# Second RMS norm of a decoder layer moved behind the gate and up products, its squares added by GpSimd, the first two output units interleaved

## The chip, the cores and the metric

One Trainium2 chip; the program runs on one of its cores. The metric is the time of one execution on the device in microseconds, here the median of three runs.

## What is computed

A two-layer hybrid decoder trunk on 320 tokens (256 of a prompt, 64 new ones of eight sequences), model width 1024. Each layer projects the normed input, runs three token mixers (a linear recurrence, latent attention over a paged cache, a gated chunk mixer), merges them with sigmoid gates, adds the result of an output projection to x, and then runs a SwiGLU feed-forward network of width 2816. The change is in this last part:

```python
x = x + jnp.sum(gates * proj, axis=2) @ lp['w_out']
hf = rms_norm(x, lp['ffn_norm'])     # x * rsqrt(mean(x*x) + EPS) * g
x = x + (jax.nn.silu(hf @ lp['w_gate']) * (hf @ lp['w_up'])) @ lp['w_down']
```

## The kernel before

Everything is feature-major: x is held as 8 tiles of 128 features by 320 tokens (KT = 8, T = 320). Each weight matrix is streamed in units of 128 x 1024 values, 129 per layer, through three slots (SLOTS). For every unit SyncE loads it into `raw`, ScalarE copies it rounded into `w_hi` and VectorE subtracts to get `w_lo` (both called `split` in the code; each is a fixed place in its engine's program). TensorE forms a product as three passes (w_hi with a_hi, w_hi with a_lo, w_lo with a_hi), so a full unit is 8 x 3 matmuls of 128 x 320, and it needs its operand a in two parts as well, a high part from ScalarE and a low part from VectorE. The split of unit u may start when unit u - 3 is done on TensorE.

The order on each engine is the order of its program; semaphores join them. The part of a layer that the change touches (`ffn` of each engine) runs as follows.

Output units (U_E, 8 of them): TensorE multiplies the merged tiles `mg_hi`, `mg_lo` by w_out, unit after unit, into PSUM banks 0 to 3. For each m, VectorE splits unit m + 2, adds the bank to x[m] (L2079) and frees the bank; ScalarE splits unit m + 2, waits for x[m] and writes its square into `tmpf`. For m = 0 TensorE waits for each merged tile in turn.

Norm (`norm(l, 1, tmpf)`): TensorE multiplies the 8 squares by a matrix of ones into bank 4 (L736), ScalarE makes rb = exp(-0.5 ln(mean + eps)) from it, each of the two functions behind a table load; VectorE multiplies x[m], the gain and rb into `tmpf` (L1686), ScalarE copies pairs of tiles into `h_hi`, VectorE subtracts into `h_lo` (L1626), and TensorE starts unit U_F, two tiles at a time as they come (`first_unit`).

Gate and up units (U_F, 44 of them, 22 pairs; a loop of 7 rounds of 3 pairs and one pair behind it): of a pair, ScalarE takes tanh of the gate unit's bank (`fth`), VectorE forms (fth + 1) x gate bank and then x up bank (`fhd`), ScalarE copies this into `hid_hi`, VectorE subtracts into `hid_lo` (each the L1182 or L1626 helper). Between these steps stand the splits of the two units ahead. The gate bank is freed after the (fth + 1) step, the up bank after the last product.

Down units (U_G, 22): each adds one hidden tile's product into all 8 banks, so that the first of them waits bank by bank for a free one; behind them VectorE adds the banks to x.

GpSimd has nothing to do in these stages; its next work is to load the vectors of the next layer.

Of the kernel before, what the change touches and what calls it, by code (L numbers as in the profile page):

```python
# [21 lines left out]
T = SEQ + TS  # L22
# [44 lines left out]
def build_program(nc, ins, outs):  # L67
# [116 lines left out]
    fhd = sb("fhd", [128, 2, T], on=st5)  # L184
    st5.close()
# [170 lines left out]
    ff_p = Signal("ffn_product", NF)  # L356
# [177 lines left out]
    def _(pool):  # L534
        nc.gpsimd.memset(ones[:], 1.0).then_inc(consts_set.sem, 1)

        with pool.Fori(0, DEPTH) as l:
# [152 lines left out]
            for q in (NB - 2, NB - 1):  # L690
                for m in range(NPG // 2):
                    if m % 2 == 0:
                        split_probabilities(q, m // 2)
                    rows_lo(q, m)


    @block.tensor
    def _(pe):
# [22 lines left out]
        def first_unit(l, u, slot, bank, n):  # L721

            pe.wait_ge(lo_done.sem, lo_done.at(l, u + 1))
            pe.wait_ge(bank_free[bank].sem, banks.take(l, bank))
            for j in range(KT // 2):
                pe.wait_ge(h_ready.sem, h_ready.at(l, 4 * n + j + 1))
# [4 lines left out]
        def norm(l, n, tmp):  # L731

            pe.wait_ge(bank_free[4].sem, banks.take(l, 4))
            for m in range(KT):
                pe.wait_ge(sq_ready.sem, sq_ready.at(l, n * KT + m + 1))
                last = mm(PS[:, 4, 0:T], ones[:], tmp[:, m, :], start=m == 0, stop=m == KT - 1)  # L736
            last.then_inc(norm_sum.sem, 1)
# [6 lines left out]
        def project(l):  # L744
            norm(l, 0, tmp8)
            first_unit(l, 0, 0, 0, 0)
# [377 lines left out]
        def ffn(l):  # L1124
            for m in range(KT):
                pe.wait_ge(lo_done.sem, lo_done.at(l, U_E + m + 1))
                pe.wait_ge(bank_free[m % 4].sem, banks.take(l, m % 4))
                for k in range(KT):
# [4 lines left out]
                done.then_inc(unit_done.sem, 1)  # L1133
            norm(l, 1, tmpf)
            with pe.Fori(0, 7) as i:
                banks.enter(i, [0, 1, 2, 3, 5, 6])
                first_unit(l, i * 6 + U_F, U_F % SLOTS, 0, 1)
                for j, b in ((1, 1), (2, 2), (3, 3), (4, 5), (5, 6)):
                    full_unit(l, i * 6 + (U_F + j), (U_F + j) % SLOTS, b)
                banks.leave(7)  # L1140
            for j in (42, 43):
                full_unit(l, U_F + j, (U_F + j) % SLOTS, j - 42)
# [37 lines left out]
    def _(act):  # L1180
# [20 lines left out]
        def norm(l, n, tmp):  # L1201
            if n == 0:
                split(l, 0)
            for m in range(KT):
                act.wait_ge(x_ready.sem, x_ready.at(l, n * KT + m + 1))
                A(tmp[:, m, :], x[:, m, :], ACT.Square).then_inc(sq_ready.sem, 1)
            act.wait_ge(norm_sum.sem, norm_sum.at(l, n + 1))
            rs(rb[:], PS[:, 4, 0:T], D).then_inc(rb_ready.sem, 1)
            release(4)
            if n == 0:  # L1210
                split(l, 1)
            for j in range(4):
                act.wait_ge(ht_ready.sem, ht_ready.at(l, 4 * n + j + 1))
                A(h_hi[:, 2 * j:2 * j + 2, :], tmp[:, 2 * j:2 * j + 2, :], ACT.Copy).then_inc(hh_ready.sem, 1)
            if n == 0:
                act.wait_ge(par_abs.sem, par_abs.at(l, 1))
                A(sm(S_E, 0, 4), sm(S_E, 0, 4), ACT.Exp, scale=-1.0).then_inc(par_exp.sem, 1)
# [24 lines left out]
        def project(l):  # L1242
            norm(l, 0, tmp8)
# [321 lines left out]
        def ffn(l):  # L1565
            for m in range(KT):
                split(l, U_E + m + 2)
                act.wait_ge(x_ready.sem, x_ready.at(l, KT + m + 1))
                if m == 0:
                    act.wait_ge(mgh.sem, mgh.at(l, 8))  # L1570
                A(tmpf[:, m, :], x[:, m, :], ACT.Square).then_inc(sq_ready.sem, 1)
            act.wait_ge(norm_sum.sem, norm_sum.at(l, 2))
            rs(rb[:], PS[:, 4, 0:T], D).then_inc(rb_ready.sem, 1)
            release(4)
            for j in range(4):
                act.wait_ge(ht_ready.sem, ht_ready.at(l, 4 + j + 1))
                A(h_hi[:, 2 * j:2 * j + 2, :], tmpf[:, 2 * j:2 * j + 2, :], ACT.Copy).then_inc(hh_ready.sem, 1)

            def hidden(fi, c, i, step, bank, s):

                u = i * step + c
                split(l, c + 2, i, step)
# [7 lines left out]

            with act.Fori(0, 7) as i:
                for j in range(3):
                    hidden(i * 3 + j, U_F + 2 * j, i, 6, (0, 2, 5)[j], j % 2)
            hidden(21, U_F + 42, 0, 0, 0, 0)
# [18 lines left out]
    def _(dve):  # L1613
# [59 lines left out]
        def norm(l, n, tmp, gain):  # L1673
            if n == 0:
                split(l, 0)
            if n == 0:
                dve.wait_ge(vec_in.sem, vec_in.at(l, 16))
            dve.wait_ge(rb_ready.sem, rb_ready.at(l, n + 1))

            def pair_lo(j):  # L1680
                dve.wait_ge(hh_ready.sem, hh_ready.at(l, 4 * n + j + 1))
                lo(h_lo[:, 2 * j:2 * j + 2, :], tmp[:, 2 * j:2 * j + 2, :], h_hi[:, 2 * j:2 * j + 2, :]).then_inc(h_ready.sem, 1)

            for j in range(4):
                for m in (2 * j, 2 * j + 1):
                    last = V.scalar_tensor_tensor(tmp[:, m, :], x[:, m, :], v(gain, m), rb[:], ALU.mult, ALU.mult)  # L1686
# [4 lines left out]
            if n == 0:  # L1691
                split(l, 1)
                lru_parameters(l)

        def project(l):

            norm(l, 0, tmp8, "attn_g")
# [581 lines left out]
```

## Time and profile before

| | us |
|---|---|
| median of three runs | 1702.2 (1700.59 to 1705.34) |
| profiled execution, its own time | 1704.65 |
| span of that execution in the trace | 1703.1 |
| TensorE matmul busy, of the span | 1611.5 (95%) |
| TensorE weight load busy | 1537.3 (90%) |
| VectorE busy | 1029.7 (60%) |
| ScalarE busy | 941.2 (55%) |
| GpSimd busy | 458.7 (27%) |
| mean granted TensorE clock | 0.986 of full |

A busy share is the share of the span in which an instruction of that engine ran. The span is that of the trace, 1.55 us shorter than the execution's own time. Matmuls are pipelined: one lasts 0.31 us and the next starts 0.147 us after it, so that busy time alone doesn't say how close TensorE is to its pace; the idle stretches before its instructions do.

### The profile page before, as it was taken

The numbers are of one execution on the slowest core, as the hardware profiler recorded it, in microseconds if no ns is written. First come the engines' busy times: TensorE is split into PE (matmuls) and PEld (weight loads), VectorE is DVE, ScalarE is ACT, GpSimd is POOL, SyncE is SP. The second block draws the span as 40 slices with busy tenths as digits, with TensorE's granted clock in tenths as the row PEclk, the third lists the DMA queues.
The fourth block names the chain that finished last, engine by engine and source line by source line (L and its number), as shares of the span: only waits on it lengthen the run. The fifth ranks groups of instructions, "written<-read, shape, count | busy, mean of one in ns | idle before, by whom it ended". The sixth has DMA issues, their size and how long they took to land.

```text
span 1703.1 us, 34614 instructions
## 1 busy us (share of the span) xinstructions
PE 1611.5 (95%) x10896; PEld 1537.3 (90%) x10896; DVE 1029.7 (60%) x1557; ACT 941.2 (55%) x1654; POOL 458.7 (27%) x519
## 2 busy tenths in 40 slices
PE   7988999999999989999989889999999999899998
PEld 6875999999999989999978669999999999899998
DVE  5566777778543655554375567777784536555533
ACT  6585777777634344443366947776775343444331
POOL 1113356766620000000012223667666100000000
PEclk9999999999999999999999989999999999999999
DMA  6321355444444434444444123645435444344443
GB/s 228 116 71 50 113 181 155 148 147 142 149 142 135 158 106 152 150 150 149 136 148 127 48 63 119 188 142 155 150 122 179 125 138 160 105 151 150 149 148 105
DMA packets 113795, 232.02 MB, mean 136 GB/s; under 512 B 12801, under 2 KB 78402, under 8 KB 113410
## 3 DMA queue, kind: packets, MB, share of 16 engines
q1 hardware_dynamic: 111458, 222.94, 41.8%
q0 software_dynamic: 2208, 7.51, 1.3%
q8 instruction: 64, 1.05, 0.3%
q14 instruction: 65, 0.53, 0.1%
HBM read 227.93 MB, written 2.46 MB: 135 GB/s over the span
## 4 chain that ended last, share of the span: by engine, by line
PE 72%; ACT 9%; DVE 6%; issue 5%; DVEq 3%; ACTq 3%; POOLq 1%; DMA 0%; POOL 0%; SPq 0%
PE PS L711 45%; PE PS L955 18%; ACT L1182 2%; PE PS L988 1%; PE PS L989 1%; PE PS L950 1%; PE PS L736 1%; ACT lt_hi L1182 1%; ACTq L1186 1%; ACT ksqp L1182 1%; DVEq L1709 1%; DVEq L1617 1%; ACT r_hi L1182 1%; DVE xc L1711 1%; POOLq L652 1%
## 5 line engine op out<-in xcount | busy, mean ns | idle before, releaser
L1623 DVE TENSOR_TENSOR w_lo<-raw,w_hi 128x1024 fp32r<-128x1024 f32 x258 | 317.0, 1229 | 287.7 <-ACT w_hi L1182 274.8
L711 PE MATMUL PS<-h_hi,w_hi 128*128 128x320 f32 x1360 | 429.9, 316 | 31.3 <-DVE h_lo L1626 20.8
L711 PE MATMUL PS<-h_lo,w_hi 128*128 128x320 f32 x1360 | 424.8, 312 | 0.0
L711 PE MATMUL PS<-h_hi,w_lo 128*128 128x320 f32 x1360 | 424.6, 312 | 0.0
L1182 ACT ACTIVATE w_hi<-raw 128x1024 fp32r<-128x1024 f32 x258 | 272.0, 1055 | 161.9 <-PE PS L711 134.4
L711 PEld LDWEIGHTS PS<-h_hi,w_hi 128*128 128x128 f32 x1360 | 259.3, 191 | 40.5 <-issue 17.1
L711 PEld LDWEIGHTS PS<-h_lo,w_hi 128*128 128x128 f32 x1360 | 259.8, 191 | 0.3
L711 PEld LDWEIGHTS PS<-h_hi,w_lo 128*128 128x128 f32 x1360 | 259.4, 191 | 0.0
L955 PE MATMUL PS<-comb_hi,lt_hi 128*128 128x288 f32 x1024 | 240.2, 315 | 0.0
L1182 ACT ACTIVATE ksqp<-PS 128x512 f32<-128x512 f32 x256 | 152.5, 596 | 145.4 <-PE PS L955 143.1
L1969 DVE TENSOR_REDUCE kss<-ksqp 128x8 f32<-128x512 f32 x256 | 172.8, 680 | 96.6 <-ACT ksqp L1182 96.2
L955 PE MATMUL PS<-comb_lo,lt_hi 128*128 128x288 f32 x1024 | 218.7, 295 | 0.0
L955 PE MATMUL PS<-comb_hi,lt_lo 128*128 128x288 f32 x1024 | 218.6, 294 | 0.0
L660 POOL TENSOR_TENSOR r_lo<-rrow,r_hi 128x512 fp32r<-128x512 f32 x128 | 167.1, 1309 | 114.7 <-ACT r_hi L1182 114.6
L955 PEld LDWEIGHTS PS<-comb_lo,lt_hi 128*128 128x128 f32 x1024 | 164.1, 188 | 0.0
L955 PEld LDWEIGHTS PS<-comb_hi,lt_lo 128*128 128x128 f32 x1024 | 163.8, 188 | 0.0
L955 PEld LDWEIGHTS PS<-comb_hi,lt_hi 128*128 128x128 f32 x1024 | 159.1, 189 | 0.0
L639 POOL TENSOR_TENSOR lt_hi<-tpage,lt_hi 64x256 fp32r<-64x256 f32 x128 | 120.5, 942 | 94.3 <-ACT lt_hi L1182 77.8
L1626 DVE TENSOR_TENSOR lt_lo<-tpage,lt_hi 128x512 fp32r<-128x512 f32 x128 | 107.4, 839 | 24.5 <-ACT lt_hi L1182 24.5
L1182 ACT ACTIVATE lt_hi<-tpage 128x768 fp32r<-128x768 f32 x128 | 108.3, 846 | 2.3 <-DMA tpage<-in_tcache 2.3
L711 PE MATMUL PS<-hid_hi,w_hi 128*128 (+1 forms) x352 | 108.5, 308 | 0.4 <-DVEq L1617 0.4
L711 PE MATMUL PS<-hid_lo,w_hi 128*128 (+1 forms) x352 | 108.3, 308 | 0.0
(293 smaller groups left out, 2646.3 us busy)
## 6 DMA issues: line engine op xcount, KB each, us to landing
raw<-in_stream SPq DMA_DIRECT2D x258, 512.0 KB, 3.5
tpage<-in_tcache SPq DMA_DIRECT2D x256, 192.0 KB, 2.4
rrow<-in_rcache SPq DMA_DIRECT2D x256, 128.0 KB, 2.6
x<-in_xT SPq DMA_DIRECT2D x2, 640.0 KB, 5.4
sbias<-in_sbias POOLq DMA_DIRECT2D x2, 640.0 KB, 6.0
out_yT<-x SPq DMA_DIRECT2D x1, 1280.0 KB, 4.5
const<-in_consts SPq DMA_DIRECT2D x1, 1088.0 KB
wgate<-in_wgate POOLq DMA_DIRECT2D x2, 512.0 KB, 3.8
```

The costliest lines, as they stand in the source:

```text
L639: nc.gpsimd.tensor_tensor(half, tpage[64:128, c % TBUF, :, 256:384], f(half), ALU.subtract).then_inc(pt_rope.sem, 1)
L652: pool.drain()
L660: nc.gpsimd.tensor_tensor(r_lo[:, at, :], rrow[:, src, :], f(r_hi[:, at, 0:KVL]), ALU.subtract).then_inc(rows_split.sem, 1)
L711: done = mm(out, w[:, slot, c], a, start=first and n == 0 and m == 0, stop=last and n == len(pairs) - 1 and m == 2)
L736: last = mm(PS[:, 4, 0:T], ones[:], tmp[:, m, :], start=m == 0, stop=m == KT - 1)
L950: mm(PS[:, rotary_bank(p, par), r0:r0 + HT], lt_hi[:, t, i, 256:384], q128_of(b), start=True, stop=True)
L955: last = mm(PS[:, 2 * s + g, c0:c0 + 288], a[:, t, i, 128 * k:128 * k + 128], w[:, k, g, c0:c0 + 288], start=k == 0 and n == 0, stop=k == ...
L988: mm(PS[:, 7, 0:KVL], w, r_lo[:, r, :], start=False, stop=False)
L1182: return nc.scalar.activation(out, in_, func, **kw)
L1623: V.tensor_tensor(w_lo[:, s, :], raw[:, s, :], f(w_hi[:, s, :]), ALU.subtract).then_inc(lo_done.sem, 1)
L1626: return V.tensor_tensor(out, whole, f(hi_), ALU.subtract)
L1969: V.tensor_reduce(kss[:, par, p, :], ksqp[:, s, :].rearrange("p (h c) -> p h c", h=H), AX.X, ALU.add).then_inc(pk_ss.sem, 1)
```

## The change

1. The operand of gate and up products is no longer the normed x but x times the gain alone: ScalarE writes `h_hi[m]` from x[m] with the gain as the scale, as soon as x[m] is there, ahead of the square; VectorE writes `h_lo[m]` = x[m] x gain - h_hi[m] in one instruction, behind the split of the next turn. h_ready counts 8 tiles, not 4 pairs.
2. TensorE runs unit U_F straight behind the output units, tile by tile, then the sum of squares, then U_F + 1, then the loop. The squares of tiles 1 to 6 are added onto that of tile 0 by GpSimd, so that TensorE has two products with the ones instead of eight.
3. The token's norm rb is applied to the banks: VectorE writes fgs = gate bank x rb and, later, fus = up bank x rb, and the hidden value is (fth + 1) x fgs x fus. The tanh reads fgs instead of the bank, so ScalarE waits for VectorE twice in a pair (`ff_p` counts two per pair).
4. The first pair stands ahead of the loop, not behind it, and the banks rotate accordingly.
5. The first two output units are interleaved: tiles 0 to 3 of both, then tiles 4 to 7 of both.

The core of the diff (ScalarE's and TensorE's other `norm` only loses its parameters):

```diff
 # GpSimd, behind the pages of the layer
+            pool.wait_ge(sq_ready.sem, sq_ready.at(l, KT + 1))
+            pool.sem_inc(waits_passed, 1)
+            for m in range(1, KT - 1):
+                pool.wait_ge(sq_ready.sem, sq_ready.at(l, KT + m + 1))
+                pool.sem_inc(waits_passed, 1)
+                nc.gpsimd.tensor_tensor(tmpf[:, 0, :], tmpf[:, 0, :], tmpf[:, m, :], ALU.add)
+                last = pool.drain()
+            last.then_inc(sq_added.sem, 1)
 # TensorE, ffn
+            for m in (0, 1):
+                output_unit_ready(m)
+                merged_product(m, range(0, 4))
+            for m in (0, 1):
+                merged_product(m, range(4, KT)).then_inc(unit_done.sem, 1)
+            for m in range(2, KT):
+                output_unit_ready(m)
+                merged_product(m, range(KT)).then_inc(unit_done.sem, 1)
+            pe.wait_ge(lo_done.sem, lo_done.at(l, U_F + 1))
+            pe.wait_ge(bank_free[0].sem, banks.take(l, 0))
+            for k in range(KT):
+                pe.wait_ge(h_ready.sem, h_ready.at(l, 4 + k + 1))
+                done = tiles(PS[:, 0, 0:T], U_F % SLOTS, [(k, h_hi[:, k, :], h_lo[:, k, :])], first=k == 0, last=k == KT - 1)
+            done.then_inc(unit_done.sem, 1)
+            pe.wait_ge(bank_free[4].sem, banks.take(l, 4))
+            pe.wait_ge(sq_added.sem, sq_added.at(l, 1))
+            mm(PS[:, 4, 0:T], ones[:], tmpf[:, 0, :], start=True, stop=False)
+            pe.wait_ge(sq_ready.sem, sq_ready.at(l, 2 * KT))
+            mm(PS[:, 4, 0:T], ones[:], tmpf[:, KT - 1, :], start=False, stop=True).then_inc(norm_sum.sem, 1)
+            full_unit(l, U_F + 1, (U_F + 1) % SLOTS, 1)
 # ScalarE, ffn
+                A(h_hi[:, m, :], x[:, m, :], ACT.Copy, scale=v("ffn_g", m)).then_inc(hh_ready.sem, 1)
                 A(tmpf[:, m, :], x[:, m, :], ACT.Square).then_inc(sq_ready.sem, 1)
+            split(l, U_F + 2)
             act.wait_ge(norm_sum.sem, norm_sum.at(l, 2))
             rs(rb[:], PS[:, 4, 0:T], D).then_inc(rb_ready.sem, 1)
 # ScalarE, hidden
-                act.wait_ge(unit_done.sem, unit_done.at(l, u + 1))
-                A(fth[:, s, :], PS[:, bank, 0:T], ACT.Tanh, scale=0.5).then_inc(ff_t.sem, 1)
+                act.wait_ge(ff_p.sem, ff_p.at(l, fi * 2 + 1))
+                A(fth[:, s, :], fgs[:, s, :], ACT.Tanh, scale=0.5).then_inc(ff_t.sem, 1)
                 split(l, c + 3, i, step)
-                act.wait_ge(ff_p.sem, ff_p.at(l, fi + 1))
+                act.wait_ge(ff_p.sem, ff_p.at(l, fi * 2 + 2))
 # VectorE, ffn and hidden
+            def h_low(m):
+                dve.wait_ge(hh_ready.sem, hh_ready.at(l, 4 + m + 1))
+                V.scalar_tensor_tensor(h_lo[:, m, :], x[:, m, :], v("ffn_g", m), f(h_hi[:, m, :]),
+                                       ALU.mult, ALU.subtract).then_inc(h_ready.sem, 1)
             for m in range(KT):
                 split(l, U_E + m + 2)
+                if m:
+                    h_low(m - 1)
                 dve.wait_ge(unit_done.sem, unit_done.at(l, U_E + m + 1))
...
                 split(l, c + 2, i, step)
-                dve.wait_ge(ff_t.sem, ff_t.at(l, fi + 1))
-                V.scalar_tensor_tensor(fth[:, s, :], fth[:, s, :], 1.0, PS[:, gb, 0:T], ALU.add, ALU.mult)
+                dve.wait_ge(unit_done.sem, unit_done.at(l, u + 1))
+                V.tensor_tensor(fgs[:, s, :], PS[:, gb, 0:T], rb[:], ALU.mult).then_inc(ff_p.sem, 1)
                 release(gb)
                 split(l, c + 3, i, step)
+                dve.wait_ge(ff_t.sem, ff_t.at(l, fi + 1))
+                V.scalar_tensor_tensor(fth[:, s, :], fth[:, s, :], 1.0, fgs[:, s, :], ALU.add, ALU.mult)
                 dve.wait_ge(unit_done.sem, unit_done.at(l, u + 2))
-                V.tensor_tensor(fhd[:, s, :], fth[:, s, :], PS[:, ub, 0:T], ALU.mult).then_inc(ff_p.sem, 1)
+                V.tensor_tensor(fus[:, s, :], PS[:, ub, 0:T], rb[:], ALU.mult)
                 release(ub)
+                V.tensor_tensor(fhd[:, s, :], fth[:, s, :], fus[:, s, :], ALU.mult).then_inc(ff_p.sem, 1)
```

## Rows read from the trace of the kernel before

**Rows 1.** The page, costliest groups: the FFN's and projections' first product.

```profile
L711 PE MATMUL PS<-h_hi,w_hi 128*128 128x320 f32 x1360 | 429.9, 316 | 31.3 <-DVE h_lo L1626 20.8
```

**Rows 2.** Chain of waits, 598 to 640 us (start, us, what).

```profile
607.15 4.32 PE PS L736 x16
...
611.50 0.53 ACT rb L1182
...
613.88 1.94 DVE tmpf L1686 x4
...
616.70 23.38 PE PS L711 x143
```

**Rows 3.** Timeline of VectorE in the output products, first layer (start, us, instruction, idle before).

```profile
581.56 1.22 DVE L1623 TENSOR_TENSOR w_lo<-raw,w_hi 128x1024 fp32r<-128x1024 f32 x1
582.70 0.48 DVE L2079 SCALAR_TENSOR_TENSOR x<-PS,x 128x320 f32<-128x320 f32 x1
...
607.19 0.49 DVE L2079 SCALAR_TENSOR_TENSOR x<-PS,x 128x320 f32<-128x320 f32 x1 [0.32 <-PE PS L711]
```

**Rows 4.** Timeline of ScalarE behind the last output product.

```profile
607.71 0.47 ACT L1182 ACTIVATE tmpf<-x 128x320 f32<-128x320 f32 x1 [2.10 <-DVE x L2079]
608.20 1.28 ACT L1182 ACT_TABLE_LOAD   x1
```

**Rows 5.** Timeline of TensorE: the two stalls beside the second norm's.

```profile
580.49 0.41 PE L711 MATMUL PS<-mg_hi,w_hi 128*128 128x320 f32 x1 [1.57 <-DVE mg_lo L1626]
...
774.61 0.41 PE L711 MATMUL PS<-hid_hi,w_hi 128*128 128x320 f32 x1 [0.18 <-DVEq L1617]
```

**Rows 6.** Timeline of VectorE in the loop over the hidden tiles.

```profile
652.24 1.23 DVE L1623 TENSOR_TENSOR w_lo<-raw,w_hi 128x1024 fp32r<-128x1024 f32 x1 [0.46 <-ACT w_hi L1182]
654.34 0.49 DVE L2092 TENSOR_TENSOR fhd<-fth,PS 128x320 f32<-128x320 f32 x1 [0.88 <-PE PS L711]
...
656.41 1.22 DVE L1623 TENSOR_TENSOR w_lo<-raw,w_hi 128x1024 fp32r<-128x1024 f32 x1 [0.33 <-ACT w_hi L1182]
```

**Rows 7.** Timeline of ScalarE in the same loop.

```profile
640.88 0.47 ACT L1182 ACTIVATE hid_hi<-fhd 128x320 f32 x1 [2.76 <-DVE fhd L2092]
641.53 1.06 ACT L1182 ACTIVATE w_hi<-raw 128x1024 fp32r<-128x1024 f32 x1 [0.18 <-issue]
...
650.82 0.44 ACT L1182 ACTIVATE fth<-PS 128x320 f32<-128x320 f32 x1 [1.48 <-PE PS L711]
651.15 1.05 ACT L1182 ACTIVATE w_hi<-raw 128x1024 fp32r<-128x1024 f32 x1
654.96 0.47 ACT L1182 ACTIVATE hid_hi<-fhd 128x320 f32 x1 [2.75 <-DVE fhd L2092]
655.34 1.04 ACT L1182 ACTIVATE w_hi<-raw 128x1024 fp32r<-128x1024 f32 x1
```

**Rows 8.** Timeline of VectorE in the branch products: a drain between, and none.

```profile
576.93 0.48 DVE L2010 SCALAR_TENSOR_TENSOR th<-th,PS 128x320 f32<-128x320 f32 x1
577.53 0.49 DVE L2012 TENSOR_TENSOR acc<-acc,th 128x320 f32<-128x320 f32 x1
577.94 0.48 DVE L2010 SCALAR_TENSOR_TENSOR th<-th,PS 128x320 f32<-128x320 f32 x1
```

**Rows 9.** ScalarE groups by shape, two column operands: xcount | busy us, mean ns | idle.

```profile
L1182 ACT ACTIVATE va<-va,vec,small 128x320 f32<-128x320 f32 x8 | 4.5, 638 | 0.0
```

**Rows 10.** Instructions of r_lo and of lt_lo: duration ns, lowest/median/highest.

```profile
L660 POOL TENSOR_TENSOR r_lo<-rrow,r_hi x128: 1178/1196/2283, 226.3 to 1326.2; 128x512 fp32r<-128x512 f32 x128
...
L1626 DVE TENSOR_TENSOR lt_lo<-tpage,lt_hi x128: 673/693/1247, 154.2 to 1272.1; 128x512 fp32r<-128x512 f32 x128
```

**Rows 11.** Busy time by stretch; the last three values are PEclk, DMA share, GB/s.

```profile
612.00:616.00 4.00, 0.00 (x0) 0.00 (x0) 2.12 (x5) 2.66 (x5) 0.00 (x0) 0.82 0.00 0
```

**Rows 12.** Chain of waits in the second layer.

```profile
1461.33 18.76 PE PS L711 x116
...
1618.58 74.20 PE PS L711 x504
```

More of the change, by code:

```diff
@@ L184, in build_program @@
     fhd = sb("fhd", [128, 2, T], on=st5)
+    fgs, fus = sb("fgs", [128, 2, T], on=st5), sb("fus", [128, 2, T], on=st5)
     st5.close()
@@ L719, in full_unit, with first_unit @@
             tiles(PS[:, bank, 0:T], slot, [(k, h_hi[:, k, :], h_lo[:, k, :]) for k in range(KT)]).then_inc(unit_done.sem, 1)
-        def first_unit(l, u, slot, bank, n):
+        def first_unit(l, u, slot, bank):
             pe.wait_ge(lo_done.sem, lo_done.at(l, u + 1))
@@ L729, in first_unit, with norm @@
             done.then_inc(unit_done.sem, 1)
-        def norm(l, n, tmp):
+        def norm(l):
             pe.wait_ge(bank_free[4].sem, banks.take(l, 4))
             for m in range(KT):
-                pe.wait_ge(sq_ready.sem, sq_ready.at(l, n * KT + m + 1))
-                last = mm(PS[:, 4, 0:T], ones[:], tmp[:, m, :], start=m == 0, stop=m == KT - 1)
+                pe.wait_ge(sq_ready.sem, sq_ready.at(l, m + 1))
+                last = mm(PS[:, 4, 0:T], ones[:], tmp8[:, m, :], start=m == 0, stop=m == KT - 1)
             last.then_inc(norm_sum.sem, 1)
@@ L744, in project @@
         def project(l):
-            norm(l, 0, tmp8)
-            first_unit(l, 0, 0, 0, 0)
+            norm(l)
+            first_unit(l, 0, 0, 0)
             full_unit(l, 1, 1, 1)
@@ L1124, in ffn, with merged_product @@
         def ffn(l):
[L1125 to L1128, printed above, removed]
+            def merged_product(m, ks):
+                for k in ks:
                     if m == 0:
@@ L1132, in ffn, with output_unit_ready @@
                                  first=k == 0, last=k == KT - 1)
-                done.then_inc(unit_done.sem, 1)
-            norm(l, 1, tmpf)
+                return done
+            def output_unit_ready(m):
+                pe.wait_ge(lo_done.sem, lo_done.at(l, U_E + m + 1))
+                pe.wait_ge(bank_free[m % 4].sem, banks.take(l, m % 4))
+            for m in (0, 1):
[18 more added lines that the diff above has]
+            full_unit(l, U_F + 1, (U_F + 1) % SLOTS, 1)
             with pe.Fori(0, 7) as i:
[L1136 to L1139, printed above, removed]
+                banks.enter(i, [2, 3, 5, 6, 0, 1])
+                for j, b in enumerate((2, 3, 5, 6, 0, 1)):
+                    full_unit(l, i * 6 + (U_F + 2 + j), (U_F + 2 + j) % SLOTS, b)
                 banks.leave(7)
-            for j in (42, 43):
-                full_unit(l, U_F + j, (U_F + j) % SLOTS, j - 42)
             def down(u, k, slot, first=False, last=False):
@@ L1199, in rs, with norm @@
             return A(out, out, ACT.Exp, scale=-0.5)
-        def norm(l, n, tmp):
-            if n == 0:
-                split(l, 0)
+        def norm(l):
+            split(l, 0)
             for m in range(KT):
-                act.wait_ge(x_ready.sem, x_ready.at(l, n * KT + m + 1))
-                A(tmp[:, m, :], x[:, m, :], ACT.Square).then_inc(sq_ready.sem, 1)
-            act.wait_ge(norm_sum.sem, norm_sum.at(l, n + 1))
+                act.wait_ge(x_ready.sem, x_ready.at(l, m + 1))
+                A(tmp8[:, m, :], x[:, m, :], ACT.Square).then_inc(sq_ready.sem, 1)
+            act.wait_ge(norm_sum.sem, norm_sum.at(l, 1))
             rs(rb[:], PS[:, 4, 0:T], D).then_inc(rb_ready.sem, 1)
             release(4)
-            if n == 0:
-                split(l, 1)
+            split(l, 1)
             for j in range(4):
[L1213 to L1217, printed above, removed]
+                act.wait_ge(ht_ready.sem, ht_ready.at(l, j + 1))
+                A(h_hi[:, 2 * j:2 * j + 2, :], tmp8[:, 2 * j:2 * j + 2, :], ACT.Copy).then_inc(hh_ready.sem, 1)
+            act.wait_ge(par_abs.sem, par_abs.at(l, 1))
+            A(sm(S_E, 0, 4), sm(S_E, 0, 4), ACT.Exp, scale=-1.0).then_inc(par_exp.sem, 1)
         def evac(l, u, bank, dst, sq):
@@ L1242, in project @@
         def project(l):
-            norm(l, 0, tmp8)
+            norm(l)
             split(l, 2)
@@ L1574, in ffn, with hidden @@
             release(4)
[L1575 to L1582, printed above, removed]
-                act.wait_ge(unit_done.sem, unit_done.at(l, u + 1))
-                A(fth[:, s, :], PS[:, bank, 0:T], ACT.Tanh, scale=0.5).then_inc(ff_t.sem, 1)
+            def hidden(fi, c, i, step, s, first=False):
+                if not first:
+                    split(l, c + 2, i, step)
+                act.wait_ge(ff_p.sem, ff_p.at(l, fi * 2 + 1))
+                A(fth[:, s, :], fgs[:, s, :], ACT.Tanh, scale=0.5).then_inc(ff_t.sem, 1)
                 split(l, c + 3, i, step)
-                act.wait_ge(ff_p.sem, ff_p.at(l, fi + 1))
+                act.wait_ge(ff_p.sem, ff_p.at(l, fi * 2 + 2))
                 dst = hid_hi[:, fi, :] if isinstance(fi, int) else hid_hi[:, bass.ds(fi, 1), :].rearrange("p o t -> p (o t)")
                 A(dst, fhd[:, s, :], ACT.Copy).then_inc(ff_h.sem, 1)
+            hidden(0, U_F, 0, 0, 0, first=True)
             with act.Fori(0, 7) as i:
                 for j in range(3):
-                    hidden(i * 3 + j, U_F + 2 * j, i, 6, (0, 2, 5)[j], j % 2)
-            hidden(21, U_F + 42, 0, 0, 0, 0)
+                    hidden(i * 3 + (1 + j), U_F + 2 + 2 * j, i, 6, (1 + j) % 2)
             with act.Fori(0, 6) as i:
@@ L1671, in lru_softplus_end, with norm @@
             V.tensor_scalar_mul(sm(S_NSP4, 0, 4), q, -4.0).then_inc(params.sem, 1)
[L1673 to L1678, printed above, removed]
+        def norm(l):
+            split(l, 0)
+            dve.wait_ge(vec_in.sem, vec_in.at(l, 16))
+            dve.wait_ge(rb_ready.sem, rb_ready.at(l, 1))
             def pair_lo(j):
-                dve.wait_ge(hh_ready.sem, hh_ready.at(l, 4 * n + j + 1))
-                lo(h_lo[:, 2 * j:2 * j + 2, :], tmp[:, 2 * j:2 * j + 2, :], h_hi[:, 2 * j:2 * j + 2, :]).then_inc(h_ready.sem, 1)
+                dve.wait_ge(hh_ready.sem, hh_ready.at(l, j + 1))
+                lo(h_lo[:, 2 * j:2 * j + 2, :], tmp8[:, 2 * j:2 * j + 2, :], h_hi[:, 2 * j:2 * j + 2, :]).then_inc(h_ready.sem, 1)
             for j in range(4):
                 for m in (2 * j, 2 * j + 1):
-                    last = V.scalar_tensor_tensor(tmp[:, m, :], x[:, m, :], v(gain, m), rb[:], ALU.mult, ALU.mult)
+                    last = V.scalar_tensor_tensor(tmp8[:, m, :], x[:, m, :], v("attn_g", m), rb[:], ALU.mult, ALU.mult)
                 last.then_inc(ht_ready.sem, 1)
@@ L1690, in norm @@
             pair_lo(3)
-            if n == 0:
-                split(l, 1)
-                lru_parameters(l)
+            split(l, 1)
+            lru_parameters(l)
         def project(l):
-            norm(l, 0, tmp8, "attn_g")
+            norm(l)
             V.memset(xpp[:, :, 0:3], 0.0)
@@ L2080, in ffn @@
                 release(m % 4)
-            norm(l, 1, tmpf, "ffn_g")
+            h_low(KT - 1)
             def hidden(fi, c, i, step, gb, ub, s):
@@ L2099, in hidden @@
                               hid_hi[:, bass.ds(fi, 1), :].rearrange("p o t -> p (o t)")).then_inc(hid.sem, 1)
+            hidden(0, U_F, 0, 0, 0, 1, 0)
             with dve.Fori(0, 7) as i:
                 for j in range(3):
-                    hidden(i * 3 + j, U_F + 2 * j, i, 6, (0, 2, 5)[j], (1, 3, 6)[j], j % 2)
-            hidden(21, U_F + 42, 0, 0, 0, 1, 0)
+                    hidden(i * 3 + (1 + j), U_F + 2 + 2 * j, i, 6, (2, 5, 0)[j], (3, 6, 1)[j], (1 + j) % 2)
             with dve.Fori(0, 6) as i:
```

13 lines of the change are left out of this document (8 added, 5 removed).

## The prediction

> **What bounds the kernel now.** I read the page first, then the chain of waits, then the timelines of the three engines over one stage, and last the granted clock by stretch. TensorE is busy for 95% of the span, and the costliest group's idle time is small against its busy time [rows 1]. So what can be won lies in its few gaps, and what can be lost is any place where another engine becomes slower than TensorE's pace. The pace: 504 matmuls in 74.20 us, 0.1472 us each [rows 12], thus 3.53 us for a unit of 24 and 7.04 us for a pair of gate and up units, as hid_hi shows from 640.88 to 654.96 over two pairs [rows 7].
>
> The second norm is the largest gap of a layer. The chain leaves TensorE at 611.47 (607.15 + 4.32), goes through ScalarE (Ln, table load, Exp: 611.50 to 613.88, 2.38 us), VectorE's products, and returns at 616.70 [rows 2]. There TensorE starts at the lower of its two levels (1.2 GHz): it had been idle since 611.47, and the granted clock of 612 to 616 is 0.82 on the mean [rows 11]. 143 matmuls took 23.38 us [rows 2] where the pace gives 21.05: 2.3 us. Two smaller gaps: 1.57 us ahead of the fifth merged tile, and 0.18 us ahead of the down products' bank 1 [rows 5].
>
> The loop over the pairs is where the other engines have room now: of a cycle of 7.04, VectorE idles 0.46, 0.88 and 0.33 for ScalarE and TensorE [rows 6], and ScalarE stands ready for 1.48 and 2.75 [rows 7]. Busy shares look ample; what counts is how many steps stand one behind the other.
>
> **Part 1, output units and the interleave.** The interleave gives TensorE four tiles of unit 1 in place of the 1.57 us stall [rows 5]. But x[0] doesn't come earlier: VectorE is in the split at 581.56 and adds x[0] 1.14 behind it, at 582.70 [rows 3], by when unit 0 is done in both orders (580.49 + 12 x 0.147). What sets x[m] from then on is a circle of ScalarE and VectorE: x to ScalarE 0.52 (607.19 to 607.71) [rows 3, 4]; h_hi to square; square to split 0.38, as hid_hi to split [rows 7]; split to w_lo 1.08 (651.15 to 652.24, 655.34 to 656.41) [rows 6, 7]; w_lo to the next VectorE step 1.14 [rows 3]; then x. Without the new steps that is 3.12, below 3.53, so that TensorE is waited for (0.32 us) [rows 3]. The change adds h_hi and h_low. h_hi has a column operand: an activation with two of them takes 638 ns [rows 9] against 470 [rows 4], so one costs 0.08 more, between none and 0.17; its step is 0.38 + 0.09 = 0.47. h_low is of the form of L1686, four in 1.94 [rows 2], 0.47 apart. The circle is 3.12 + 0.47 + 0.47 = 4.06, over TensorE's 3.53. x[7] comes at 582.70 + 7 x 4.06 = 611.1 and not at 607.19: 3.9 us lost, and the interleave is worth nothing. TensorE is ahead of the circle by a unit or more and feels it only in the last two or three units.
>
> **Part 2, the norm.** x[7] 611.12; h_hi 611.64 to 612.20; h_low to 612.8; three matmuls and two sum products of two passes each at 4.32 / 16 = 0.27 [rows 2]: sum at 614.65. ScalarE: square 612.11, split 612.49 to 613.54, table load of 1.28 [rows 4] to 614.8. GpSimd's six additions lie beside all this: one has 4.06 us, and its nearest row is a subtraction of 128x512 with 1178 ns [rows 10]. rb is ready 2.38 later, so fgs of pair 0 starts at 617.2. What is taken away: four product steps, the pair copies and h_lo behind rb, six sum products (3.2 us) and U_F at the low level, which now runs ahead of rb. GpSimd's queue holds only the next layer's vectors behind the additions, which nobody needs for long.
>
> **Part 3, the loop.** The rescale puts ScalarE's tanh behind a VectorE step, and two steps more ahead of hid_hi. I follow the waits round one pair: split A to w_lo A 1.07; to fgs 1.14; fgs to tanh 0.52 (as x to square); tanh to split B 0.38, for it now reads SBUF (0.33 from PSUM) [rows 7]; to w_lo B 1.09; to the (fth + 1) step 1.14; to fus 0.41 (577.53 to 577.94); through the drain to fhd 0.60 (576.93 to 577.53) [rows 8]; to hid_hi 0.62 (654.34 to 654.96) [rows 6, 7]; to the next split A 0.38. Sum 7.35. At the end of a loop round ScalarE needs 0.65 in place of 0.38 between hid_hi and split (640.88 to 641.53) [rows 7]: 0.27, six times between seven rounds. TensorE asks for 7.04. So the circle is now slower than TensorE by 0.31 a pair, and it doesn't contain TensorE at all. Before, tanh lay beside split A and w_lo A, and the circle was near 4.8.
>
> Of the chain's steps, those of fgs and fus are not in the trace; their nearest row is fhd (SBUF x PSUM, 0.49) [rows 6], and a two-input step can't be below the 0.41 that two of them stand apart. Bounds for the circle: 7.25 (overlaps of 0.05 at two places) to 7.45 (0.05 more at two).
>
> **Sum.** fus of pair 0 is 0.52 + 0.38 + 1.08 + 1.14 + 0.41 = 3.53 behind fgs, at 620.76. fus of pair 21 is at 620.76 + 21 x 7.35 + 6 x 0.27 = 776.7, its bank is free 0.60 later, at 777.3; that is when the down products go on to bank 1, now 774.61 [rows 5]. Layer one: +2.7. In layer two the stage starts 844.63 later (616.70 to 1461.33) [rows 2, 12]: 1622.0 against 1618.58 [rows 12], +3.4. Behind it nothing changes: TensorE alone sets the pace of the 22 down units. Together +6.1. One unknown: TensorE has then been idle for about 3 us (it ends unit 43 near 773 and has three matmuls). A gap of 1.57 ahead of 580.49 was followed by the full level, one of 5.2 by the low one, at a price of 2.3. I take half of it, 1.15 a layer, between 0 and 2.3. Total +8.4: span 1711.5, the execution 1713.0 (1.55 outside the span) against its 1704.65; that execution was 2.45 over the median, so on the median 1710.6.
>
> **Rivals.**
> Faster: the circle is not longer than TensorE's pace, because handovers overlap more than the pitches of before tell; it decides at 7.04 for the mean, loop ends included (I have 7.43), so it needs 0.4 less a pair. Then the norm's gain stays: with the circle exactly at the pace, bank 1 is free at 620.76 + 147.84 + 0.60 = 769.2, and with a faster one at 766.5 (U_F + 1 ends near 618.0), 5.4 to 8.1 less in layer one and 0.7 less of a gain in layer two. That is 10 to 16 us: 1690. For it speaks that VectorE's share is only 60%; against it, that each link is a measured pitch.
> Balanced: the circle's mean is 7.2 to 7.35 and the clock stays up. 0.1 a pair is 2.1 a layer, 4.2 in all; 1700 to 1707.
> Slower still: GpSimd's additions collide with VectorE. Rows show such pairs: r_lo goes from 1178 to 2283 ns and lt_lo from 673 to 1247 [rows 10], a step waiting out nearly another. An addition starts some 1.6 us behind x[m] and takes 0.74 to 1.18 (r_lo by elements, or whole), and w_lo starts 2.45 behind x[m]: up to 0.35 in the circle, six times, up to 2.1 a layer: 1715.
> The Trainium skill ("SBUF — State Buffer", section "Who interferes with whom") speaks against the change here: a VectorE instruction with two SBUF inputs and a GpSimd one that reads SBUF block each other for the whole instruction, whichever started first. By that rule the collision is as just worked out, and the trace's stretched r_lo and lt_lo agree; without it the term is 0.
>
> **How the numbers follow.** The forecast of 1710.5 has a chance of 0.51, with a range of its own from 1705 to 1716 (circle 0.1 shorter or longer with the clock's term to the other side); GpSimd 0.10; balanced 0.25; faster 0.14. A measurement of this kernel tells 0.3% (5.1 us) from no change: below 1697.1 is faster, above 1707.3 slower. Slower: 0.43 of the forecast's 0.51 and 0.10, 0.53. Same: 0.25 and 0.08, 0.33. Faster 0.14. The range of 1695 to 1718 leaves out most of the faster case and little above.
>
> **What would show it.** In the changed kernel: x[1] to x[7] about 4.05 apart, with VectorE no longer waiting for TensorE there; rb ready near 617; fgs to fgs 7.35 and 7.62 at loop ends, with w_lo of split A as what TensorE waits for once in a pair, some 0.3 us; a gap of some 3 us inside the first down unit until fus's bank is released. If instead fgs waits for TensorE in each pair and the period is 7.04, part 3 is wrong and the time falls below 1697. If x[m] come 3.53 apart, part 1 is. If the 3 us gap is followed by matmuls 0.27 apart, the clock's term is the full one.

## The result and the profile after

The changed kernel takes 1712.5 us (median of 5 runs, 1709.8 to 1717.6), the kernel before in the same session 1703.4 (5 runs). The ratio is 1.0063 with a 95% interval of 1.0048 to 1.0077: slower by 0.6%, or 9.1 us. 1710.5 had been forecast.

The profiled execution took 1709.82 (span 1708.3), the lowest of the five, while that of before was 2.4 above the median that was shown with it. Total spans therefore tell less than stretches. In all traces of this study the work ahead of the output units varies by some microseconds from execution to execution, so I count from x[0], the first tile that VectorE adds in the output units, to the start of the first matmul on bank 1 in the down units.

| | before, layer 1 | after, layer 1 | before, layer 2 | after, layer 2 |
|---|---|---|---|---|
| x[0] | 582.70 | 580.51 | 1427.33 | 1427.21 |
| x[7] | 607.19 | 608.75 | 1451.82 | 1455.44 |
| last product of pair 0 (fhd) | 626.18 | 619.03 | 1470.15 | 1465.73 |
| last product of pair 21 | 774.02 | 775.56 | 1617.99 | 1622.25 |
| down units go on to bank 1 | 774.61 | 775.52 | 1618.58 | 1622.21 |
| from x[0] to there | 191.91 | 195.01 | 191.25 | 195.00 |

The table reads in three steps. x[7] comes 3.75 later against x[0]. Pair 0 is nevertheless done 5.0 earlier in layer 1 (38.52 behind x[0], not 43.48; in layer 2 4.3, for there it was 42.82 before), which is the norm's gain less what the output units lost. Then the 21 further pairs take 156.5 and not 147.8. Bank 1 is now free as fhd starts and not behind it, so that of the 3.7 us between these 3.1 remain as a loss (layer 2: 3.75).

The page of the kernel after: the row of TensorE (busy, share, count) and the chain that ended last, by engine.

```profile
PE 1615.7 (95%) x10872; PEld 1531.5 (90%) x10872; DVE 1053.6 (62%) x1637; ACT 945.3 (55%) x1662; POOL 471.3 (28%) x531
...
PE 51%; ACT 17%; DVEq 11%; DVE 8%; issue 8%; ACTq 4%; POOLq 1%; POOL 0%; DMA 0%
```

TensorE is busy for as large a share as before, and that says nothing: its share of the chain fell from 72% to 51%, and ScalarE (9% to 17%), VectorE (6% to 8%) and VectorE's sequencer, DVEq, which issues the releases of banks (3% to 11%), took it.

Timeline of VectorE in the output units of the kernel after (start, us, instruction, what it waited for), to be laid beside [rows 3].

```profile
584.54 0.49 DVE L2108 SCALAR_TENSOR_TENSOR x<-PS,x 128x320 f32<-128x320 f32 x1
586.97 1.23 DVE L1648 TENSOR_TENSOR w_lo<-raw,w_hi 128x1024 fp32r<-128x1024 f32 x1 [1.94 <-ACT w_hi L1211]
588.11 0.55 DVE L2100 SCALAR_TENSOR_TENSOR h_lo<-x,vec,h_hi 128x320 fp32r<-128x320 f32 x1
588.57 0.49 DVE L2108 SCALAR_TENSOR_TENSOR x<-PS,x 128x320 f32<-128x320 f32 x1
```

x to x is 4.03. There is no wait for TensorE left as in the last row of [rows 3]; what VectorE waits for is ScalarE's split, 1.94 in each turn.

Timeline of VectorE over a pair and to the end of the next, at a loop end, beside [rows 6]; then ScalarE's, beside [rows 7]. Split A is that of the next pair's gate unit, split B that of its up unit.

```profile
633.91 0.49 DVE L2126 TENSOR_TENSOR fhd<-fth,fus 128x320 f32<-128x320 f32 x1
...
636.00 1.23 DVE L1648 TENSOR_TENSOR w_lo<-raw,w_hi 128x1024 fp32r<-128x1024 f32 x1 [0.32 <-ACT w_hi L1211]
637.14 0.48 DVE L2118 TENSOR_TENSOR fgs<-PS,rb 128x320 f32<-128x320 f32 x1
639.11 1.23 DVE L1648 TENSOR_TENSOR w_lo<-raw,w_hi 128x1024 fp32r<-128x1024 f32 x1 [1.49 <-ACT w_hi L1211]
640.26 0.48 DVE L2122 SCALAR_TENSOR_TENSOR fth<-fth,fgs 128x320 f32<-128x320 f32 x1
640.66 0.48 DVE L2124 TENSOR_TENSOR fus<-PS,rb 128x320 f32<-128x320 f32 x1
641.26 0.49 DVE L2126 TENSOR_TENSOR fhd<-fth,fus 128x320 f32<-128x320 f32 x1
...
648.98 0.49 DVE L2126 TENSOR_TENSOR fhd<-fth,fus 128x320 f32<-128x320 f32 x1
```

```profile
637.66 0.47 ACT L1211 ACTIVATE fth<-fgs 128x320 f32<-128x320 f32 x1 [1.69 <-DVE fgs L2118]
638.04 1.04 ACT L1211 ACTIVATE w_hi<-raw 128x1024 fp32r<-128x1024 f32 x1
641.88 0.47 ACT L1211 ACTIVATE hid_hi<-fhd 128x320 f32 x1 [2.80 <-DVE fhd L2126]
642.63 1.06 ACT L1211 ACTIVATE w_hi<-raw 128x1024 fp32r<-128x1024 f32 x1 [0.27 <-issue]
```

From one last product (fhd) to the next it is 7.35 (633.91 to 641.26), and 7.72 across the end of a loop round (641.26 to 648.98). One can walk round the circle in these rows: split A at 636.00, fgs 1.14 later, tanh at 637.66, split B at 638.04 and 639.11, the (fth + 1) step 1.15 later, fus 0.40, fhd 0.60, hid_hi at 641.88. Nowhere does VectorE or ScalarE wait for TensorE; in [rows 6] and [rows 7] they did.

The chain of waits at both ends of the loop, beside [rows 2].

```profile
612.25 3.53 PE PS L721 x24
...
775.52 14.56 PE PS L721 x87
```

TensorE goes from the norm's sum into unit U_F + 1 at the full pace, 24 matmuls in 3.53, where 143 took 23.38 before [rows 2]. So TensorE begins the loop's first unit, U_F + 2, 35.1 behind x[0] (at 615.61), and 43.3 before: a gain of 8.2. The loop takes it back: TensorE begins the first down unit at 772.03, 191.52 behind x[0], and 191.12 before. The circle's lag is thus lost inside the loop, 8.6 spread over the pairs, and what is left as the loss of the whole stage comes behind it.

Timeline of TensorE at the first down unit; then busy time by stretch (PEclk, DMA share, GB/s last).

```profile
775.52 0.42 PE L721 MATMUL PS<-hid_hi,w_hi 128*128 128x320 f32 x1 [2.78 <-DVEq L1642]
...
776.51 0.47 PE L721 MATMUL PS<-hid_hi,w_hi 128*128 128x320 f32 x1
```

```profile
776.00:779.00 3.00, 3.00 (x15) 3.00 (x14) 1.76 (x3) 1.53 (x2) 0.00 (x0) 0.58 0.52 172
```

2.78 us of waiting for bank 1 (0.18 before), and from 776.51 on 12 matmuls 0.267 apart in place of 0.147: the granted clock of the stretch (TensorE's clock as a share of full speed) is 0.58 on the mean, TensorE was at the lower of its two levels (1.2 GHz) there. The price is 12 x 0.12 = 1.4 us, and in layer 2 the same. Unit 43 is done by then; VectorE, held by the slower circle, has yet to read the last pair's banks.

### The profile page after: what moved, and what is told of

It is laid out like the page before. It is cut to its first block, busy times and chain, and to the rows that moved or that the text cites. A ratio compares the mean times of both kernels' runs of the same rounds, so it can differ in the third digit from the quotient of the medians.

```text
span 1708.3 us, 34692 instructions
## 1 busy us (share of the span) xinstructions
PE 1615.7 (95%) x10872; PEld 1531.5 (90%) x10872; DVE 1053.6 (62%) x1637; ACT 945.3 (55%) x1662; POOL 471.3 (28%) x531
## 4 chain that ended last, share of the span: by engine, by line
PE 51%; ACT 17%; DVEq 11%; DVE 8%; issue 8%; ACTq 4%; POOLq 1%; POOL 0%; DMA 0%
PE PS L721 25%; PE PS L965 17%; DVEq L1642 9%; ACT w_hi L1211 7%; ACT L1211 2%; DVE fhd L2126 1%; PE PS L998 1%; PE PS L999 1%; PE PS L960 1%; ACT lt_hi L1211 1%; ACT ksqp L1211 1%; DVE w_lo L1648 1%; DVE fus L2124 1%; ACT r_hi L1211 1%; ACTq L1215 1%
## 5 line engine op out<-in xcount | busy, mean ns | idle before, releaser
L721 PE MATMUL PS<-hid_hi,w_lo 128*128 (+1 forms) x352 | 110.1, 313 | 0.0
```

The lines of the kernel that those rows point to most:

```text
L721: done = mm(out, w[:, slot, c], a, start=first and n == 0 and m == 0, stop=last and n == len(pairs) - 1 and m == 2)
```

## The experiments

The theory: in each stage a circle of ScalarE and VectorE steps, one released by the other, competes with TensorE's pace; the longer of the two sets the time. The change lengthened the circle to 4.03 in the output units (TensorE 3.53) and to 7.34 in the loop (TensorE 7.04), and this costs more than the norm gains. The rivals: the added instructions cost time as work on VectorE; the interleave or GpSimd's additions do it; the loss lies somewhere else and only shows at the down units. Times are medians; the ratio is to the kernel before in the same session.

**The interleave alone, in the kernel before.**

```diff
-            for m in range(KT):
...
+            for m in (0, 1):
+                output_unit_ready(m)
+                merged_product(m, range(0, 4))
+            for m in (0, 1):
+                merged_product(m, range(4, KT)).then_inc(unit_done.sem, 1)
+            for m in range(2, KT):
+                output_unit_ready(m)
+                merged_product(m, range(KT)).then_inc(unit_done.sem, 1)
```

> The kernel before with part 5 alone: the first two output units interleaved. Circle theory (x[m] is paced by the longer of TensorE's unit, 3.53 us, and the circle of ScalarE and VectorE, 3.12 us in the kernel before): x[0] stays where it is, but x[7] follows TensorE, which is 1.6 to 1.7 us ahead: 1.6 a layer faster, 3.2 in all, about 1700 against 1703.4. Rival (the interleave never pays, since VectorE's split holds x[0]): 0.

Measured: 1698.6, ratio 0.9977 (0.9965 to 0.9990), 3.9 us faster by the ratio. Timeline of VectorE, x[0], x[1] and x[7]:

```profile
580.77 0.49 DVE L2090 SCALAR_TENSOR_TENSOR x<-PS,x 128x320 f32<-128x320 f32 x1
...
583.88 0.48 DVE L2090 SCALAR_TENSOR_TENSOR x<-PS,x 128x320 f32<-128x320 f32 x1
...
603.51 0.49 DVE L2090 SCALAR_TENSOR_TENSOR x<-PS,x 128x320 f32<-128x320 f32 x1 [0.31 <-PE PS L711]
```

x[0] to x[1] is 3.11, the short circle of before, until it has caught up with TensorE; x[7] comes 22.74 behind x[0] in place of 24.49. So x[7] gains 1.75 a layer by the interleave where the circle is shorter than TensorE's unit. From x[0] to bank 1 this execution gained less, 1.3 and 0.5 (190.61 and 190.73): behind the norm about 18 and 20 matmuls ran at the lower level, and about 15 and 10 in the execution of before. The time agrees with the theory's 3.2 within its interval (1.7 to 6.0) and not with the rival's zero.

**The rescale alone, in the kernel before.** The factor is a tile of ones.

```diff
+                V.tensor_tensor(fgs[:, s, :], PS[:, gb, 0:T], one[:], ALU.mult).then_inc(ff_p.sem, 1)
+                release(gb)
...
-                V.scalar_tensor_tensor(fth[:, s, :], fth[:, s, :], 1.0, PS[:, gb, 0:T], ALU.add, ALU.mult)
+                V.scalar_tensor_tensor(fth[:, s, :], fth[:, s, :], 1.0, fgs[:, s, :], ALU.add, ALU.mult)
...
+                V.tensor_tensor(fus[:, s, :], PS[:, ub, 0:T], one[:], ALU.mult)
```

> The kernel before with the rescale of the loop alone (fgs and fus, tanh of fgs), the factor being a tile of ones, so that nothing else moves. Circle theory: fus of pair 0 stands where fhd of pair 0 stood (626.2), then 21 x 7.34 + 6 x 0.38, and bank 1 is free at 783.2 and not 774.6: 8.6 a layer, with 1.4 for the clock behind the gap ahead of the down products 10 a layer: about 1723, 20 above the kernel before. Rival (the rescale is only extra work on an engine that is 60% busy, and the loss of the changed kernel lies in its output products or norm): 0 to 4.

Measured: 1723.6, ratio 1.0108 (1.0092 to 1.0124), 18.4 by the ratio and 20.7 by the medians. Timeline of VectorE, the last products of three pairs in a row:

```profile
631.35 0.49 DVE L2098 TENSOR_TENSOR fhd<-fth,fus 128x320 f32<-128x320 f32 x1
...
638.69 0.49 DVE L2098 TENSOR_TENSOR fhd<-fth,fus 128x320 f32<-128x320 f32 x1
...
646.32 0.49 DVE L2098 TENSOR_TENSOR fhd<-fth,fus 128x320 f32<-128x320 f32 x1
```

7.34 to the next, 7.63 across a loop end. From x[0] to bank 1 it is 199.69 and 200.39 in the two layers, 7.8 and 9.1 more than before. The loss is in the loop, and the time lost is about twice what the whole change loses: the norm gives the rest back. The loop end costs 0.28 here and not the 0.38 of the expectation, which is the changed kernel's.

**The same instructions in another order.** The split A that stood at the start of the next pair is put ahead of hid_hi and hid_lo of this one. VectorE's first one goes ahead of the loop, and the splits for the down units behind the loop move up by one.

```diff
 # ScalarE; VectorE likewise, between fhd and hid_lo
-                if not first:
-                    split(l, c + 2, i, step)
                 act.wait_ge(ff_p.sem, ff_p.at(l, fi * 2 + 1))
                 A(fth[:, s, :], fgs[:, s, :], ACT.Tanh, scale=0.5).then_inc(ff_t.sem, 1)
                 split(l, c + 3, i, step)
+                split(l, c + 4, i, step)
                 act.wait_ge(ff_p.sem, ff_p.at(l, fi * 2 + 2))
```

> The changed kernel with the split of the next gate unit moved on both engines: ScalarE does it ahead of hid_hi and VectorE ahead of hid_lo, not behind them. Same instructions, same number. Circle theory: a pair's split A leaves the circle, which is then some 6.1 us, below 7.04; TensorE sets the pace, unit 43 ends near 763.6 and bank 1 is free at 764.3, not 775.5: 11.3 a layer and 1.4 of clock: 25 below the changed kernel, about 1687, 16 below the kernel before. Rival (VectorE's added instructions themselves cost the time): no change against the changed kernel, 1712.

Measured: 1684.2, ratio 0.9891 (0.9872 to 0.9911). This is the run that decides: no work was taken away from VectorE, and 28 us went. The traces have 11.3 a layer from x[0] to bank 1 (183.7 for 195.0) and, with no matmul at the lower level there, 1.4 of clock: 25.5, as forecast. Chain of waits; then timeline of VectorE (two fgs in a row) and of ScalarE.

```profile
611.81 147.86 PE PS L721 x1008
763.78 26.23 PE PS L721 x177
```

```profile
661.13 0.49 DVE L2117 TENSOR_TENSOR fgs<-PS,rb 128x320 f32<-128x320 f32 x1 [0.79 <-PE PS L721]
...
668.17 0.49 DVE L2117 TENSOR_TENSOR fgs<-PS,rb 128x320 f32<-128x320 f32 x1 [0.80 <-PE PS L721]
```

```profile
669.08 1.04 ACT L1211 ACTIVATE w_hi<-raw 128x1024 fp32r<-128x1024 f32 x1
671.69 1.06 ACT L1211 ACTIVATE w_hi<-raw 128x1024 fp32r<-128x1024 f32 x1 [1.57 <-PE PS L721]
672.92 0.47 ACT L1211 ACTIVATE hid_hi<-fhd 128x320 f32 x1 [0.17 <-DVE fhd L2125]
```

1008 matmuls stand in one piece of the chain, 147.86 us. fgs to fgs is 7.04, and fgs and the moved split (671.69) both wait for TensorE again.

**Both stages in another order.** In the output units, too, the split of the next weight unit goes ahead of the steps that only serve h.

```diff
 # ScalarE; VectorE likewise, ahead of h_low
+            split(l, U_E + 2)
             for m in range(KT):
-                split(l, U_E + m + 2)
+                if m < KT - 1:
+                    split(l, U_E + m + 3)
                 act.wait_ge(x_ready.sem, x_ready.at(l, KT + m + 1))
```

> The run above, and in the output units each split of a weight unit moved ahead of h_hi and the square on ScalarE and ahead of h_low on VectorE (for tile 7 behind them, as before). Circle theory: x[m] follows TensorE at 3.53 in place of 4.03, the interleave's 1.6 comes through, and unit U_F + 1 ends 4.6 earlier against x[0]: 9 below the run above, about 1678. Rival (once the loop follows TensorE, the stretch ahead of it is hidden): 1687, the same as the run above.

Measured: 1678.9, ratio 0.9844 (0.9825 to 0.9862). Against the run before it 4.4 us a layer are gained from x[0] to bank 1 (179.3 for 183.7), 8.8 in all for 9 forecast; the time has 5.3 by the medians and 8.0 by the ratios. Either is far from the rival's zero. Chain of waits:

```profile
599.90 10.55 PE PS L721 x72
611.54 147.85 PE PS L721 x1008
```

Apart from the four passes of the sum, TensorE runs from the output units to unit U_F + 43 without a gap.

**The changed kernel without the interleave.** The edit is the reverse of the first one.

> The changed kernel without part 5: the output units one after the other. Circle theory: x[m] is paced by a circle of 4.03 us, so TensorE's 1.6 us don't come through: no change against the changed kernel (within 1 us). Rival (the interleave is worth in both kernels what it was alone, about 4): 4 slower.

Measured: 1712.2, ratio 1.0059 (1.0046 to 1.0072). No change, as the theory had it: x[7] stands 28.22 behind x[0], with the interleave 28.24, and bank 1 follows x[0] by 194.98 in layer 1, with it by 195.01 (in layer 2 by 196.32 for 195.00; that is the clock, told of at the end).

**Both reorderings without the interleave, twice.**

> Both reorderings, without part 5. Circle theory: now TensorE paces the output products again and the stall of 1.6 us a layer is on the path: 3.2 above the run with both reorderings, about 1682. Rival (never on the path): 0.

Measured: 1679.7, ratio 0.9878 (0.9864 to 0.9893): 0.8 above the run with the interleave by the medians, 5.8 by the ratios, of different sessions. That left it open, so both kernels were run once more side by side.

> The kernel of both reorderings again, beside the next, so that what the interleave is worth there is told on one chip in one session. The traces so far have, from x[0] to bank 1 of the down products, 179.7 with and 181.4 without it. If that is what the time shows: 3.5 below the next run.

> Both reorderings without the interleave, again: 3.5 above the run beside it by the circle theory and the traces; 0.8 if the medians of the two earlier sessions were the truth.

Measured: 1677.1 with (ratio 0.9870, 0.9854 to 0.9887), 1681.2 without (0.9894, 0.9877 to 0.9910). 4.0 apart, and no execution of the one is as slow as the fastest of the other (1676.3 to 1679.7, 1681.0 to 1683.6); the traces have 1.75 a layer. (The expectation's 179.7 and 181.4 count to the end of the first matmul on bank 1; to its start, as above, it is 179.3 and 181.0.) So the interleave is worth nothing in the changed kernel and 4 us behind the reorderings: the same edit, with another thing ending last.

**Eight sums on TensorE in place of GpSimd's additions.** On top of both reorderings.

```diff
-            pe.wait_ge(sq_added.sem, sq_added.at(l, 1))
-            mm(PS[:, 4, 0:T], ones[:], tmpf[:, 0, :], start=True, stop=False)
-            pe.wait_ge(sq_ready.sem, sq_ready.at(l, 2 * KT))
-            mm(PS[:, 4, 0:T], ones[:], tmpf[:, KT - 1, :], start=False, stop=True).then_inc(norm_sum.sem, 1)
+            for m in range(KT):
+                pe.wait_ge(sq_ready.sem, sq_ready.at(l, KT + m + 1))
+                last = mm(PS[:, 4, 0:T], ones[:], tmpf[:, m, :], start=m == 0, stop=m == KT - 1)
+            last.then_inc(norm_sum.sem, 1)
```

> Both reorderings, with eight products with the ones on TensorE in place of GpSimd's six additions and two products. TensorE runs without a gap there, so six products of 0.54 come on top: 3.2 a layer, 6.5 in all, about 1685. Rival (GpSimd's additions hold up VectorE's h_lo, 1.17 us in place of 0.55, and cost as much as they save): 0.

Measured: 1684.0, ratio 0.9894 (0.9880 to 0.9909), 5 above by the medians (of another session), and from x[0] to bank 1 182.5 for 179.3, 3.2 a layer. That is the price of six products, as forecast, so GpSimd's additions pay by the products that they replace; the rival's zero is out.

**Only the order of the banks in the first down unit, in the changed kernel.**

```diff
-                for m in range(KT):
+                order = (2, 3, 4, 5, 6, 7, 0, 1) if first else range(KT)
+                for m in order:
...
-                    if m == KT - 1:
+                    if m == order[-1]:
```

> The changed kernel with one edit: the first down unit takes the banks in the order 2 to 7, 0, 1, so that its 18 matmuls on free banks run while VectorE still reads the last pair's. If the circle's lag is paid in the gap of 2.8 us ahead of the down products and in the lower clock behind it (1.4), both go: 4 a layer, 8 below the changed kernel, about 1704. Rival (the lag is inside the loop and only shows there): 0 to 1.

Measured: 1705.0, ratio 1.0021 (1.0007 to 1.0034): 7.5 below the changed kernel. Timeline of TensorE, its only wait there:

```profile
774.64 0.41 PE L721 MATMUL PS<-hid_hi,w_hi 128*128 128x320 f32 x1 [0.43 <-DVEq L1643]
```

0.43 in place of 2.78, and no matmuls at the lower level behind it: the second down unit starts 195.5 behind x[0] (775.19), in the changed kernel 199.7 (780.24) and before 195.1 (777.79). The loop is as slow as in the changed kernel (156.5 from the last product of pair 0 to that of pair 21), so the circle's lag is still there and still cancels the norm's gain. What went is what it caused behind the loop, a wait and the lower level, and that was most of the net loss (7.5 of 9.1). Reordering the loop removes the lag itself and gives 28.

## Why the prediction was right

**The output units.** The circle was worked out as 4.06, and it is 4.03; x[7] is 28.24 behind x[0] for 28.42. "The interleave is worth nothing" holds in the changed kernel and, as its condition said, only there.

**The norm.** fgs of pair 0 was put 34.5 behind x[0] (617.2 less 582.70) and starts at 614.90, 34.39 behind. The column operand's price, taken as half of what two cost [rows 9], came out so: h_hi takes 0.56 against 0.47.

**The loop.** 7.35 forecast, 7.34 to 7.35 measured, though two of the links (fgs, fus) were not in the trace and were priced by the nearest row. The term that was mis-sized is the loop end: 0.27 by [rows 7], 0.37 here, six times; 0.6 a layer too little. The row had been read rightly, for in the run with the rescale alone, whose loop is laid out as before, it is 0.28; what makes it dearer in the changed loop stays open. The step from pair 0, now ahead of the loop, to pair 1 takes 7.54, which no term stood for.

**The end.** +2.7 and +3.4 were forecast for bank 1, +3.1 and +3.75 measured; the loop end makes up the difference. The clock's term was half of 2.3 and is 1.4. That it came so near is luck: half was a choice between nothing and the full price, and behind the same wait of 2.79 in the run with the rescale alone about 21 and 11 matmuls ran at the lower level, not 12. Sum: 6.85 and 2.8 or so, 9.7 for 8.4; by the medians 9.1.

**The rivals.** The faster case needed the handovers to overlap more, and a mean of 7.04 or less, loop ends included: it is 7.45 (156.53 in 21 steps), so they don't. That the time falls below the kernel before once the circle is shorter than 7.04, the third run shows, but by another order, not by more overlap. The collision of GpSimd with VectorE had a chance of 0.10. In the changed kernel it doesn't happen:

```profile
586.17 0.88 POOL L702 TENSOR_TENSOR tmpf<-tmpf 128x320 f32<-128x320 f32 x1 [105.66 <-ACT tmpf L1211]
```

All but 0.1 us of the addition (to 587.05) lies between x[1] (to 585.03) and the split at 586.97, in VectorE's idle time, and h_lo takes 0.55 as it would alone.

**The signature in the loop.** TensorE was to wait some 0.3 once in each pair for w_lo of split A. In the list of waits this hardly shows: between 620 and 775 it has 6 waits of TensorE for w_lo, 2.5 us, and 7.9 us of weight loads that waited for nothing the profile names ("issue"). The starts of the matmuls show it. Timeline of TensorE inside a round, and at the loop end behind it:

```profile
637.04 0.31 PE L721 MATMUL PS<-h_hi,w_lo 128*128 128x320 f32 x1
637.39 0.41 PE L721 MATMUL PS<-h_hi,w_hi 128*128 128x320 f32 x1
637.63 0.30 PE L721 MATMUL PS<-h_lo,w_hi 128*128 128x320 f32 x1
...
644.38 0.31 PE L721 MATMUL PS<-h_hi,w_lo 128*128 128x320 f32 x1
645.11 0.41 PE L721 MATMUL PS<-h_hi,w_hi 128*128 128x320 f32 x1 [0.42 <-DVE w_lo L1648]
```

The two steps beside the matmul at 637.39 are 0.35 and 0.24 in place of 0.147 each: 0.30 lost, and the matmul starts 0.16 behind the end of w_lo of split A (636.00 + 1.23). At the loop end it is 0.68. Each layer has such a place at the gate unit of every pair from pair 2 on; with 0.4 ahead of the first down unit they make up the 8.6. The kernel before and the run with the loop reordered have none. So this signature held, in size too.

## What to carry to other kernels

When a step is moved from one engine to another inside a pipelined loop, follow the waits round one turn and add up the start-to-start pitches; compare this circle with the pace of the bound engine, and don't look at busy shares (VectorE was at 60%). If the circle is longer, look for a step on it that only feeds the bound engine (here a weight split) and issue it ahead of the one that waits: here the same instructions then cost nothing. A wait behind such a loop can be filled with work that is ready, which took away most of the net loss here, but not the lag in the loop. And an edit that removes a stall is worth what ends last after it: the interleave was worth 0 or 4 us by that alone.

## What was not expected of the hardware

GpSimd and VectorE held each other up as soon as the output units were reordered. In that order GpSimd's addition and VectorE's h_lo start almost together; in the changed kernel they don't overlap, and take 0.88 and 0.55. The instructions of h_lo and of the addition (duration ns, lowest/median/highest); then one pair of them on the two timelines; then h_lo of the run without GpSimd's additions.

```profile
L2100 DVE SCALAR_TENSOR_TENSOR h_lo<-x,vec,h_hi x16: 545/1168/1171, 586.3 to 1440.2; 128x320 fp32r<-128x320 f32 x16
...
L702 POOL TENSOR_TENSOR tmpf<-tmpf x12: 962/1005/1007, 588.4 to 1437.6; 128x320 f32<-128x320 f32 x12
```

```profile
588.57 1.17 DVE L2100 SCALAR_TENSOR_TENSOR h_lo<-x,vec,h_hi 128x320 fp32r<-128x320 f32 x1
```

```profile
588.43 0.97 POOL L702 TENSOR_TENSOR tmpf<-tmpf 128x320 f32<-128x320 f32 x1 [104.65 <-ACT tmpf L1211]
```

```profile
L2091 DVE SCALAR_TENSOR_TENSOR h_lo<-x,vec,h_hi x16: 544/547/551, 586.3 to 1439.2; 128x320 fp32r<-128x320 f32 x16
```

h_lo went from 547 to 1168 ns, by 0.62, and the addition from 0.88 to 1.0; without the additions h_lo is at 547 again, so the additions are the cause. The Trainium skill ("SBUF — State Buffer", section "Who interferes with whom") has it that a VectorE instruction with two SBUF inputs and a GpSimd one that reads SBUF contend for a port pair that is locked by one of them at a time. The trace agrees that they hold each other up, but the hold is shorter than the whole instruction of the prediction: with all of h_lo's 0.55 behind the addition's end (589.40) it would end at 589.95, and it ends at 589.74. It cost no time here, for the circle of the output units had room: x[7] is 22.74 behind x[0] with the additions and without them, and TensorE has no gap in that stretch.

The clock differed between executions of one stretch. In the changed kernel the gaps of 1.4 and 0.9 us ahead of the norm's sum were followed by matmuls at the full level, in both layers (granted clock 1.00). In the second layer of the run with only the bank order changed the same gaps were followed by the lower level, and pair 0 came 1.2 later; so it was, with gaps of 1.3 and 0.9, in the second layer of the changed kernel without the interleave (1.3 later). Busy time by stretch in the run with the bank order, behind the second gap:

```profile
1454.00:1458.00 4.00, 3.88 (x12) 3.08 (x13) 1.29 (x2) 2.70 (x4) 0.00 (x0) 0.57 0.47 128
```

What decided it stays open.
